# Summing the squares of a hidden state on TensorE alone instead of with VectorE's adds, and two small matmul loops written as one

## The chip, the cores and the metric

The kernel runs on one core of a Trainium2 chip. The metric is the device time of one execution in microseconds (us): before the change the median of three executions is 1692.14 us (1687.17 to 1692.53). Less is better.

## The reference

One inference step of a decoder layer over 512 prompt tokens and 32 sample tokens (8 sequences of 4 tokens), 544 token columns in all, in fp32. What matters here is the end of the layer and one place inside the RWKV-7 branch:

```
def rms_norm(x, g):
    xf = x.astype(jnp.float32)
    y = xf * lax.rsqrt(jnp.mean(xf * xf, axis=-1, keepdims=True) + RMS_EPS)
    return (y * g.astype(jnp.float32)).astype(x.dtype)

def merge_ffn(x, o_nsa, o_rwkv, o_mem, mg, ...):
    g = jax.nn.sigmoid(mg)                      # three gates per channel
    m = g[:, :, 0] * (o_nsa @ w_o_nsa) + g[:, :, 1] * (o_rwkv @ w_o_rwkv) + g[:, :, 2] * (o_mem @ w_o_mem)
    x = x + m @ w_out
    hf = rms_norm(x, ffn_norm)
    return x + (jax.nn.silu(hf @ w_gate) * (hf @ w_up)) @ w_down

y = rms_norm(merge_ffn(...), final_norm)

def rwkv_scan(s0, r, decay, k, v, kk, a):       # s: one 64 x 64 state per head
    sa = jnp.einsum('bhij,bhj->bhi', s, -kk_t)
    s = s * w_t + sa * (kk_t * a_t) + v_t * k_t
    y_t = jnp.einsum('bhij,bhj->bhi', s, r_t)
```

Both RMS norms need, for each token, the sum of squares over the 1024 channels. The RWKV branch is computed in chunks; the 32 sample tokens are the last chunk, and their two products with the old state (with r and with -kk) come from separately loaded states.

## The kernel before

Activations lie transposed, channels on the 128 partitions and tokens along the row: `x1T` holds the hidden state as 8 tiles (KT = 8) of 128 x 544. Each of the engines runs one long written-out program, and they are held together by counting semaphores; nothing reorders them. All weights stream through a ring of five slots in SBUF (`sb_ring`); each slot is 128 x 1024 fp32 (512 KB), serves eight 128 x 128 weight tiles, and is refilled by SyncE once its last matmul has counted up `slot_used`. PSUM is four accumulators `acc[0..3]` of two banks; a product over 544 tokens is two matmuls of 272 columns, one for each bank. In the trace an fp32 matmul call appears as two weight loads (LDWEIGHTS) and two MATMUL instructions, one for each pass.

The end of the layer has four stages: the branch outputs are projected and merged (L1599); the output projection (L1621), 8 tiles j of 16 matmul calls; gate and up of the feed-forward (L1641), 22 pairs of tiles; and the down projection (L1665, its last tile j = 7 at L1676), 8 tiles of 44 calls.

After output-projection tile j, VectorE adds it into `x1T` (`add(j)`, L2474), ScalarE makes the scaled copy `hT` (L2015) and the square `sqT` (L2011). The sum over the 8 tiles is then made by two engines. Square 0 goes into half 0 of `sqT`, squares 1 to 7 all into half 1. For j = 1 to 6 VectorE adds half 1 onto half 0 (`add_square`, L2480), counting `sq_added`, and ScalarE may write the next square only after that. TensorE then sums over the partitions with a 128 x 128 tile of ones: `square_sum(0)` for the half 0, `square_sum(1)` for square 7, each one call for each bank of `acc[3]` (L1610). ScalarE makes the reciprocal root from `acc[3]` (L2018, L2019). For the last norm the same is done with the down projection's tiles, and `square_sum(0)` and the halves of `square_sum(1)` stand inside and after the last tile, which is computed one bank after the other so that the final scaling (L2526) of the first 272 tokens can start early.

In the RWKV branch, TensorE also carries "fill" matmuls of the input projections (L935) between small matmuls that wait on other engines. For the sample chunk the state products `w_s` (64 x 64 for each head; 32 rows with r, 32 rows with z) are placed by identity matmuls: the z rows into `acc[1]` (L1147, weights: a 32 x 32 identity, 64 columns moving) and the r rows, turned, into `acc[2]` (L1151, weights: 32 x 64 of `w_s`, 32 columns moving). `crossed()` goes through the 12 heads with e (the half of the partitions) alternating. `from_uv` (L1052) adds onto `acc[1]` and waits for `ws_mm`, which the last L1151 counts.

Of the kernel before, what the change touches and what calls it, by code (L numbers as in the profile page):

```python
# [260 lines left out]
def program(nc, A):  # L261
    with ExitStack() as ctx:
# [166 lines left out]
        def r_z(feats, i, t0, n):  # L429
# [69 lines left out]
        mg_sig, mg_mm, mg_part, x1_added, sqT_made, sq_added, sqT_summed, rms_inv, hf_done, gu_scaled, gu_act, up_scaled, ff_done, dn_mm, out_stored = map(  # L499
            sem, ("mg_sig", "mg_mm", "mg_part", "x1_added", "sqT_made", "sq_added", "sqT_summed", "rms_inv",  # L500
# [351 lines left out]
        def _(pe):  # L852
# [292 lines left out]
            for e, s, k, i in crossed():  # L1145
                z_rows = slice(e * HD + TS, (e + 1) * HD)
                pe.matmul(acc[1][rows[1 - e], s, k * C:(k + 1) * C], ident[z_rows, z_rows], w_s[z_rows, i, :],  # L1147
                          start=k == 0, stop=False, skip_group_check=True)
            for e, s, k, i in crossed():
                r_rows = slice(e * HD, e * HD + TS)  # L1150
                mm = pe.matmul(acc[2][feats[e], s, k * C:k * C + TS], w_s[r_rows, i, :], ident[r_rows, r_rows],  # L1151
                               start=k == 0, stop=False, skip_group_check=True)
# [455 lines left out]
            def square_sum(x, halves=(0, 1)):  # L1608
                for b in halves:
                    mm = pe.matmul(acc[3][:, b, 0:HALF_T], ones, sqT[:, x, b * HALF_T:(b + 1) * HALF_T],  # L1610
                                   start=x == 0, stop=x == 1)
# [12 lines left out]
            pe.wait_ge(sq_added, KT - 2)  # L1624
            square_sum(0)
            pe.wait_ge(sqT_made, KT)
            square_sum(1)


# [26 lines left out]
            for j in range(KT - 1):  # L1656
                if j >= 2:
                    pe.wait_ge(x1_added, KT + j - 1)
                for k in range(FFT):
# [10 lines left out]
                    elif k == FFT - 1:  # L1670
                        mm.then_inc(dn_mm, 1)
            pe.wait_ge(x1_added, KT + KT - 2)
            for b in range(2):
                for k in range(FFT):
# [3 lines left out]
                    if b == 0 and k == FFT // 2:  # L1678
                        pe.wait_ge(sq_added, 2 * (KT - 2))
                        square_sum(0)  # L1680
                    if b == 1 and k == FFT // 2:
                        pe.wait_ge(sqT_made, 2 * KT)
                        square_sum(1, (0,))
                mm.then_inc(dn_mm, 1)
            pe.wait_ge(sqT_made, 2 * KT + 1)
            square_sum(1, (1,))

        @block.scalar
        def _(act):
# [318 lines left out]
            def square(j, done, cols=slice(0, T)):  # L2008
                if j >= 2:
                    act.wait_ge(sq_added, done * (KT - 2) // KT + j - 1)  # L2010
                act.activation(sqT[:, min(j, 1), cols], x1T[:, j, cols], ACT.Square).then_inc(sqT_made, 1)  # L2011
# [5 lines left out]
            act.wait_ge(sqT_summed, 2)  # L2017
# [18 lines left out]
            for b in range(2):  # L2036
# [3 lines left out]
                act.wait_ge(sqT_summed, 4 + b)  # L2040
# [6 lines left out]
        def _(dve):  # L2047
# [428 lines left out]
            def add_square(j, done):  # L2476
                dve.wait_ge(sqT_made, done + j + 1)
                if j >= 2:
                    dve.wait_ge(sq_added, done * (KT - 2) // KT + j - 1)
# [70 lines left out]
```

## Time and profile before

| | us |
|---|---|
| median of three executions | 1692.14 |
| the profiled execution | 1692.53 |
| its span, first to last instruction | 1690.7 |
| TensorE busy in it | 1605.8 (95%) |
| VectorE busy | 454.1 (27%) |
| ScalarE busy | 382.3 (23%) |

The profiled execution is the slowest of the three shown; 1.8 us of its time lie outside the span. Busy time of an engine is the union of its instructions. A matmul's duration in the trace is longer than its distance to the next, since matmuls are pipelined: 272 columns are listed with 392 ns, yet follow each other more closely. The page's groups are summed over the whole run; the order of events at one place is read from the timeline, and what released each step from the chain of waits.

### The profile page before, as it was taken

Reading aid. Unit: us, or ns where it says so; the run is one execution under the profiler, and the core shown is the slowest. Engines: PE = TensorE matmul, PEld = TensorE weight load, DVE = VectorE, ACT = ScalarE, POOL = GpSimd, SP = SyncE. Lnnn points to the kernel's source line nnn. Section 1 sums busy time; section 2 is a strip of 40 time slices with the busy share of each in tenths; the row PEclk is TensorE's granted clock in tenths of the full one; section 3 lists DMA queues with packets and bytes.
Section 4 is the critical chain, followed back from the end, with each engine's and each line's share of the span. In section 5 each row is a group of like instructions: output and inputs, shape, how many; then the busy total and the mean of one; then the engine's idle time right before and its main releaser. Section 6 shows DMA issues by size and latency. Waiting matters only on the chain.

```text
span 1690.7 us, 30991 instructions
## 1 busy us (share of the span) xinstructions
PE 1605.8 (95%) x13440; PEld 1250.0 (74%) x13440; DVE 454.1 (27%) x915; ACT 382.3 (23%) x730; POOL 103.2 (6%) x186
## 2 busy tenths in 40 slices
PE   6999999999999999998888779999999999999997
PEld 5888578867776767875556558878788888888886
DVE  2112005523223236314664242221111111110002
ACT  3011145122222214115665432001200000000002
POOL 0000000011001003005000310000000000000000
PEclk9999999999999999999999999999999999999999
DMA  5221353321101236436000875312222222222221
GB/s 206 73 75 62 112 196 98 112 58 40 38 25 41 78 110 205 129 120 193 10 1 9 274 265 192 128 65 73 66 71 75 75 70 67 74 75 74 65 75 53
DMA packets 56445, 161.79 MB, mean 96 GB/s; under 512 B 7136, under 2 KB 20544, under 8 KB 55136
## 3 DMA queue, kind: packets, MB, share of 16 engines
q1 hardware_dynamic: 47744, 120.87, 22.4%
q0 software_dynamic: 7136, 35.73, 6.2%
q10 hardware_dynamic: 1440, 3.33, 0.5%
q8 instruction: 102, 1.67, 0.4%
q14 instruction: 23, 0.19, 0.0%
HBM read 141.91 MB, written 22.15 MB: 97 GB/s over the span
## 4 chain that ended last, share of the span: by engine, by line
PE 89%; ACT 3%; issue 2%; SPq 2%; DVE 2%; DMA 1%; ACTq 0%; DVEq 0%
PE acc L1641 19%; PE acc L935 17%; PE acc L884 9%; PE acc L1665 8%; PE acc L1599 7%; PE acc L1621 3%; PE acc L921 2%; PE acc L1030 2%; PE acc L909 2%; PE acc L1384 1%; PE acc L1371 1%; PE acc L1395 1%; PE acc L1044 1%; SPq L630 1%; PE acc L1284 1%
## 5 line engine op out<-in xcount | busy, mean ns | idle before, releaser
L935 PE MATMUL acc<-sb_work,sb_ring 128*128 128x272 f32 x1280 | 333.3, 403 | 0.6 <-ACT sb_work L1748 0.6
L1641 PE MATMUL acc<-sb_work,sb_ring 128*128 128x272 f32 x1408 | 322.8, 392 | 0.0
L1641 PEld LDWEIGHTS acc<-sb_work,sb_ring 128*128 128x128 f32 x1408 | 267.5, 190 | 55.1
L935 PEld LDWEIGHTS acc<-sb_work,sb_ring 128*128 128x128 f32 x1280 | 231.4, 190 | 57.2 <-issue 10.4
L884 PE MATMUL acc<-sb_work,sb_ring 128*128 128x272 f32 x640 | 148.8, 396 | 3.8 <-DVE sb_work L2060 3.8
L884 PEld LDWEIGHTS acc<-sb_work,sb_ring 128*128 128x128 f32 x640 | 122.7, 192 | 29.7 <-issue 4.2
L1665 PE MATMUL acc<-sb_work,sb_ring 128*128 128x272 f32 x616 | 141.3, 392 | 0.0
L1665 PEld LDWEIGHTS acc<-sb_work,sb_ring 128*128 128x128 f32 x616 | 117.0, 190 | 24.1
L2025 ACT ACTIVATE sb_work<-sb_work (+1 forms) x22 | 14.4, 657 | 277.4 <-DVE sb_work L2498 277.4
L1748 ACT ACTIVATE sb_work<-acc 128x272 f32<-128x272 f32 x80 | 31.4, 394 | 163.0 <-PE acc L935 155.7
L2474 DVE TENSOR_TENSOR sb_work<-acc,sb_work 128x544 f32<-128x544 f32 (+1 forms) x17 | 11.7, 691 | 191.8 <-PE acc L1665 132.8
L1621 PE MATMUL acc<-sb_work,sb_ring 128*128 128x272 f32 x256 | 58.9, 393 | 1.7 <-DVEq L2469 1.7
L1794 ACT ACTIVATE sb_work<-acc 128x768 f32<-128x768 f32 (+3 forms) x50 | 37.1, 743 | 101.0 <-PE acc L1044 89.2
L1621 PEld LDWEIGHTS acc<-sb_work,sb_ring 128*128 128x128 f32 x256 | 48.6, 190 | 12.1 <-DVEq L2469 2.1
L2156 DVE TENSOR_TENSOR sb_work<-acc,sb_cst 128x384 f32<-128x384 f32 (+1 forms) x41 | 22.6, 552 | 129.5 <-PE acc L1030 129.5
L2500 DVE TENSOR_TENSOR sb_work<-acc,sb_work 128x544 f32<-128x544 f32 x22 | 15.9, 724 | 143.0 <-PE acc L1641 143.0
L2498 DVE TENSOR_TENSOR sb_work<-acc,sb_work 128x544 f32 (+1 forms) x22 | 15.9, 725 | 134.5 <-PE acc L1641 134.5
L2292 DVE TENSOR_REDUCE sb_small<-acc 128x2 f32<-128x256 f32 (+3 forms) x48 | 39.5, 824 | 35.3 <-PE acc L1374 35.3
L2011 ACT ACTIVATE sb_work<-sb_work 128x544 f32<-128x544 f32 (+1 forms) x17 | 10.6, 621 | 156.3 <-DVE sb_work L2480 98.2
L1599 PE MATMUL acc<-sb_onsaT,sb_ring 128*128 128x272 f32 x192 | 45.3, 392 | 0.0
L1599 PE MATMUL acc<-sb_work,sb_ring 128*128 128x272 f32 x192 | 45.3, 392 | 0.0
L1716 ACT ACTIVATE sb_work<-acc,sb_work 128x544 f32<-128x544 f32 x20 | 14.3, 713 | 132.2 <-PE acc L884 132.2
(376 smaller groups left out, 1898.3 us busy)
## 6 DMA issues: line engine op xcount, KB each, us to landing
sb_ring<-w_stream SPq DMA_DIRECT2D x158, 512.0 KB, 3.5
sb_work<-pages SPq DMA_DIRECT2D x64, 192.0 KB, 3.7
branch_gates<-sb_work SPq DMA_DIRECT2D x24, 272.0 KB, 4.4
sb_work<-branch_gates POOLq DMA_DIRECT2D x8, 816.0 KB, 14.6
sb_work<-mem_kT SPq DMA_DIRECT2D x8, 512.0 KB, 6.6
sb_work<-mem_v SPq DMA_DIRECT2D x8, 512.0 KB, 8.7
query_features<-sb_work SPq DMA_DIRECT2D x10, 272.0 KB, 4.3
sb_work<-x_T ACTq DMA_DIRECT2D x8, 272.0 KB, 4.7
```

The source lines that it names most:

```text
L884: mm = pe.matmul(acc[n % 4][:, b, 0:HALF_T], w[:, k, :], hT[:, k, b * HALF_T:(b + 1) * HALF_T], start=k == 0, stop=k == KT - 1)
L909: mm = pe.matmul(acc[n][:, h, :], memT[:, k, n * P:(n + 1) * P], w[:, 4 * h:4 * h + 4, :].rearrange("p a c -> p (a c)"), start=k == 0, sto ...
L921: mm = pe.matmul(acc[a][:, b, 0:HALF_T], lhsT, rhs[:, b * HALF_T:(b + 1) * HALF_T], start=True, stop=True)
L935: mm = pe.matmul(acc[3][:, half, 0:HALF_T], fill_w[0][:, k, :], hT[:, k, half * HALF_T:(half + 1) * HALF_T], start=k == 0, stop=k == KT - 1)
L1030: mm = pe.matmul(acc[0][rows[1 - e], s, k * C:k * C + n], gram[rows[e], par, e, i, n:2 * n], X(par, i)[rows[e], 0:n], start=True, stop=True)
L1599: mm = pe.matmul(acc[n % 4][:, b, 0:HALF_T], w[:, block % KT, :], x[:, b * HALF_T:(b + 1) * HALF_T], start=k == 0, stop=k == len(source) - 1)
L1621: mm = pe.matmul(acc[j % 2][:, b, 0:HALF_T], w[:, k, :], mT[:, k, b * HALF_T:(b + 1) * HALF_T], start=k == 0, stop=k == KT - 1)
L1641: mm = pe.matmul(acc[2 * x + n % 2][:, b, 0:HALF_T], w[:, k, :], hT[:, k, b * HALF_T:(b + 1) * HALF_T], start=k == 0, stop=k == KT - 1)
L1665: mm = pe.matmul(acc[j % 2][:, b, 0:HALF_T], w[:, block % KT, :], ffT[:, k, b * HALF_T:(b + 1) * HALF_T], start=k == 0, stop=k == FFT - 1)
L1748: act.activation(fill_now[:, f % 2, half * HALF_T:(half + 1) * HALF_T], acc[3][:, half, 0:HALF_T], ACT.Copy, scale=scale).then_inc(fill_ou ...
L1794: act.activation(XX[0:2 * n, c % 2, first:, :, 0:n], acc[0][0:2 * n, first:, 0:PAIRS * C].rearrange("p x (i c) -> p x i c", c=C)[:, :, :, ...
L2292: dve.tensor_reduce(small[:, c:c + 2], acc[u % 2][:, :, 0:(t + 1) * P], AX, ALU.max, negate=True)\
```

## The change

1. VectorE's `add_square` and the semaphore `sq_added` are gone. Square j goes to half j % 2 of `sqT`. TensorE calls `square_sum(j)` for every j, accumulating over eight calls for each bank in `acc[3]`: in the output projection after tile j + 1 (the last one after that of j = 6), in the down projection after tile j + 1 up to j = 5; `square_sum(6)` and the two halves of `square_sum(7)` keep their places in and after the last tile. ScalarE's square j waits until `square_sum(j - 2)` is done.
2. The two loops over `crossed()` at L1147 and L1151 become one, so that for each head the z matmul and then the r matmul are issued.

```diff
@@ -496,8 +496,8 @@
         wkv_sum = sem("wkv_sum")
         y_stored, in_back = sem("y_stored"), sem("in_back")
         spilled, sig_in = [sem("spilled0"), sem("spilled1")], [sem(f"sig_in{n}") for n in range(5)]
-        mg_sig, mg_mm, mg_part, x1_added, sqT_made, sq_added, sqT_summed, rms_inv, hf_done, gu_scaled, gu_act, up_scaled, ff_done, dn_mm, out_stored = map(
-            sem, ("mg_sig", "mg_mm", "mg_part", "x1_added", "sqT_made", "sq_added", "sqT_summed", "rms_inv",
+        mg_sig, mg_mm, mg_part, x1_added, sqT_made, sqT_summed, rms_inv, hf_done, gu_scaled, gu_act, up_scaled, ff_done, dn_mm, out_stored = map(
+            sem, ("mg_sig", "mg_mm", "mg_part", "x1_added", "sqT_made", "sqT_summed", "rms_inv",
                   "hf_done", "gu_scaled", "gu_act", "up_scaled", "ff_done", "dn_mm", "out_stored"))
         two = lambda name: [sem(f"{name}{n}") for n in range(2)]
         k_in, v_in, mk_in, mv_in = map(two, ("k_in", "v_in", "mk_in", "mv_in"))
@@ -1143,11 +1143,9 @@
             pe.wait_ge(ws_out, PAIRS)
             settle()
             for e, s, k, i in crossed():
-                z_rows = slice(e * HD + TS, (e + 1) * HD)
+                r_rows, z_rows = slice(e * HD, e * HD + TS), slice(e * HD + TS, (e + 1) * HD)
                 pe.matmul(acc[1][rows[1 - e], s, k * C:(k + 1) * C], ident[z_rows, z_rows], w_s[z_rows, i, :],
                           start=k == 0, stop=False, skip_group_check=True)
-            for e, s, k, i in crossed():
-                r_rows = slice(e * HD, e * HD + TS)
                 mm = pe.matmul(acc[2][feats[e], s, k * C:k * C + TS], w_s[r_rows, i, :], ident[r_rows, r_rows],
                                start=k == 0, stop=False, skip_group_check=True)
             mm.then_inc(ws_mm, 1)
@@ -1605,10 +1603,11 @@
                             mm.then_inc(mg_mm, 1)
 
 
-            def square_sum(x, halves=(0, 1)):
+            def square_sum(j, done, count=None, halves=(0, 1)):
+                pe.wait_ge(sqT_made, count or done + j + 1)
                 for b in halves:
-                    mm = pe.matmul(acc[3][:, b, 0:HALF_T], ones, sqT[:, x, b * HALF_T:(b + 1) * HALF_T],
-                                   start=x == 0, stop=x == 1)
+                    mm = pe.matmul(acc[3][:, b, 0:HALF_T], ones, sqT[:, j % 2, b * HALF_T:(b + 1) * HALF_T],
+                                   start=j == 0, stop=j == KT - 1)
                 mm.then_inc(sqT_summed, 1)
 
             pe.wait_ge(mg_part, 3 * KT + 1)
@@ -1621,10 +1620,9 @@
                         mm = pe.matmul(acc[j % 2][:, b, 0:HALF_T], w[:, k, :], mT[:, k, b * HALF_T:(b + 1) * HALF_T],
                                        start=k == 0, stop=k == KT - 1)
                 mm.then_inc(slot_used, 1)
-            pe.wait_ge(sq_added, KT - 2)
-            square_sum(0)
-            pe.wait_ge(sqT_made, KT)
-            square_sum(1)
+                if j:
+                    square_sum(j - 1, 0)
+            square_sum(KT - 1, 0)
 
 
             def ff_tile(n, it=None):
@@ -1669,6 +1667,8 @@
                         mm.then_inc(slot_used, 1)
                     elif k == FFT - 1:
                         mm.then_inc(dn_mm, 1)
+                if j:
+                    square_sum(j - 1, KT)
             pe.wait_ge(x1_added, KT + KT - 2)
             for b in range(2):
                 for k in range(FFT):
@@ -1676,14 +1676,11 @@
                     mm = pe.matmul(acc[1][:, b, 0:HALF_T], w[:, (block + k) % KT, :], ffT[:, k, b * HALF_T:(b + 1) * HALF_T],
                                    start=k == 0, stop=k == FFT - 1)
                     if b == 0 and k == FFT // 2:
-                        pe.wait_ge(sq_added, 2 * (KT - 2))
-                        square_sum(0)
+                        square_sum(KT - 2, KT)
                     if b == 1 and k == FFT // 2:
-                        pe.wait_ge(sqT_made, 2 * KT)
-                        square_sum(1, (0,))
+                        square_sum(KT - 1, KT, 2 * KT, (0,))
                 mm.then_inc(dn_mm, 1)
-            pe.wait_ge(sqT_made, 2 * KT + 1)
-            square_sum(1, (1,))
+            square_sum(KT - 1, KT, 2 * KT + 1, (1,))
 
         @block.scalar
         def _(act):
@@ -2006,15 +2003,15 @@
                 act.activation(sg, sg, ACT.Sigmoid).then_inc(mg_sig, 1)
 
             def square(j, done, cols=slice(0, T)):
-                if j >= 2:
-                    act.wait_ge(sq_added, done * (KT - 2) // KT + j - 1)
-                act.activation(sqT[:, min(j, 1), cols], x1T[:, j, cols], ACT.Square).then_inc(sqT_made, 1)
+                if done + j >= 2:
+                    act.wait_ge(sqT_summed, done + j - 1)
+                act.activation(sqT[:, j % 2, cols], x1T[:, j, cols], ACT.Square).then_inc(sqT_made, 1)
 
             for j in range(KT):
                 act.wait_ge(x1_added, j + 1)
                 act.activation(hT[:, j, :], x1T[:, j, :], ACT.Copy, scale=v("ffn", j)).then_inc(hf_done, 1)
                 square(j, 0)
-            act.wait_ge(sqT_summed, 2)
+            act.wait_ge(sqT_summed, KT)
             own(act.activation(h2(rms), acc[3][:, :, 0:HALF_T], ACT.Ln, scale=1.0 / D, bias=stat[:, 20:21]))
             act.activation(rms, rms, ACT.Exp, scale=-0.5).then_inc(rms_inv, 1)
 
@@ -2037,7 +2034,7 @@
                 cols = slice(b * HALF_T, (b + 1) * HALF_T)
                 act.wait_ge(x1_added, 2 * KT + b)
                 square(KT - 1, KT, cols)
-                act.wait_ge(sqT_summed, 4 + b)
+                act.wait_ge(sqT_summed, 2 * KT + b)
                 own(act.activation(rms[:, cols], acc[3][:, b, 0:HALF_T], ACT.Ln, scale=1.0 / D, bias=stat[:, 20:21]))
                 act.activation(rms[:, cols], rms[:, cols], ACT.Exp, scale=-0.5).then_inc(rms_inv, 1)
                 if b == 0:
@@ -2473,18 +2470,10 @@
                 x = h2(x1T[:, j, :])[:, columns, :]
                 dve.tensor_tensor(x, acc[j % 2][:, columns, 0:HALF_T], x, ALU.add).then_inc(x1_added, 1)
 
-            def add_square(j, done):
-                dve.wait_ge(sqT_made, done + j + 1)
-                if j >= 2:
-                    dve.wait_ge(sq_added, done * (KT - 2) // KT + j - 1)
-                dve.tensor_tensor(sqT[:, 0, :], sqT[:, 0, :], sqT[:, 1, :], ALU.add).then_inc(sq_added, 1)
-
             dve.wait_ge(in_back, 80)
             for j in range(KT):
                 dve.wait_ge(slot_used, S_OUT + j + 1)
                 add(j)
-                if j >= 2:
-                    add_square(j - 1, 0)
 
             dve.sem_inc(gu_scaled, 2)
             dve.sem_inc(up_scaled, 2)
@@ -2515,9 +2504,6 @@
                 else:
                     dve.wait_ge(dn_mm, j + 1 - (j + 1) // 4)
                 add(j)
-                if j >= 2:
-                    add_square(j - 1, KT)
-            add_square(KT - 2, KT)
 
             def final(b):
                 cols = slice(b * HALF_T, (b + 1) * HALF_T)
```

TensorE in the RWKV sample chunk, before. `acc1` and `acc2` are the PSUM accumulators, L935 the fill matmuls, L1052 `from_uv`; the last number pair is output partitions x columns.

```order
L935 MATMUL acc3<-sb_work,sb_ring 128x272 [waits fill_out]
L935 MATMUL acc3<-sb_work,sb_ring 128x272 x5
L1147 MATMUL acc1<-sb_work,sb_cst 32x64 [waits ws_out]
L1147 MATMUL acc1<-sb_work,sb_cst 32x64 x11
L1151 MATMUL acc2<-sb_cst,sb_work 64x32 x12
L1052 MATMUL acc1<-sb_work 32x64 [waits ws_mm]
```

The same place after the change, from the fill matmul on; the pair of rows with acc2 and acc1 goes on until each has stood 12 times, and then L1052 follows:

```order
L935 MATMUL acc3<-sb_work,sb_ring 128x272 [waits fill_out]
L935 MATMUL acc3<-sb_work,sb_ring 128x272 x5
L1147 MATMUL acc1<-sb_work,sb_cst 32x64 [waits ws_out]
L1149 MATMUL acc2<-sb_cst,sb_work 64x32
L1147 MATMUL acc1<-sb_work,sb_cst 32x64
```

The 12 matmuls into acc1 and the 12 into acc2, two runs before, now alternate one by one.

TensorE at the end of the output projection (L1621; `w_in_slot` is a slot of the weight ring, `x1_added` the add that frees the accumulator, `sq_added` an `add_square`), before:

```order
L1621 MATMUL acc0<-sb_work,sb_ring 128x272 [waits x1_added,w_in_slot0]
L1621 MATMUL acc0<-sb_work,sb_ring 128x272 x15
L1621 MATMUL acc1<-sb_work,sb_ring 128x272 [waits x1_added,w_in_slot1]
L1621 MATMUL acc1<-sb_work,sb_ring 128x272 x15
L1610 MATMUL acc3<-sb_work 128x272 [waits sq_added]
L1610 MATMUL acc3<-sb_work 128x272
L1610 MATMUL acc3<-sb_work 128x272 [waits sqT_made]
L1610 MATMUL acc3<-sb_work 128x272
L1646 UNCONDITIONAL_BRANCH [waits hf_done]
L1646 ISA
```

After (L1620 is the output projection, L1609 the sum of squares):

```order
L1620 MATMUL acc0<-sb_work,sb_ring 128x272 [waits x1_added,w_in_slot0]
L1620 MATMUL acc0<-sb_work,sb_ring 128x272 x15
L1609 MATMUL acc3<-sb_work 128x272 [waits sqT_made]
L1609 MATMUL acc3<-sb_work 128x272
L1620 MATMUL acc1<-sb_work,sb_ring 128x272 [waits x1_added,w_in_slot1]
L1620 MATMUL acc1<-sb_work,sb_ring 128x272 x15
L1609 MATMUL acc3<-sb_work 128x272 [waits sqT_made]
L1609 MATMUL acc3<-sb_work 128x272
L1609 MATMUL acc3<-sb_work 128x272 [waits sqT_made]
L1609 MATMUL acc3<-sb_work 128x272
L1644 UNCONDITIONAL_BRANCH [waits hf_done]
L1644 ISA
```

Where one pair of square sums waited for VectorE's `sq_added` and one for ScalarE's last square, there is now a pair behind every tile but the first, each behind a wait for a square, and two pairs behind the last tile.

VectorE in the output projection (L2474 `add`, L2480 `add_square`), before:

```order
L2464 TENSOR_TENSOR sb_work<-acc2,sb_work 128x544 [waits mg_mm]
L2468 TENSOR_TENSOR sb_work<-sb_work 128x544 [waits mg_part]
L2464 TENSOR_TENSOR sb_work<-acc3,sb_work 128x544 [waits slot_used,dve_own]
L2468 TENSOR_TENSOR sb_work<-sb_work 128x544 [waits mg_part]
L2474 TENSOR_TENSOR sb_work<-acc0,sb_work 128x544 [waits dve_own,slot_used,in_back]
L2474 TENSOR_TENSOR sb_work<-acc1,sb_work 128x544 [waits slot_used]
L2474 TENSOR_TENSOR sb_work<-acc0,sb_work 128x544 [waits slot_used]
```

After:

```order
L2461 TENSOR_TENSOR sb_work<-acc2,sb_work 128x544 [waits mg_mm]
L2465 TENSOR_TENSOR sb_work<-sb_work 128x544 [waits mg_part]
L2461 TENSOR_TENSOR sb_work<-acc3,sb_work 128x544 [waits slot_used,dve_own]
L2465 TENSOR_TENSOR sb_work<-sb_work 128x544 [waits mg_part]
L2471 TENSOR_TENSOR sb_work<-acc0,sb_work 128x544 [waits dve_own,slot_used,in_back]
L2471 TENSOR_TENSOR sb_work<-acc1,sb_work 128x544 [waits slot_used]
```

The adds onto the square sum, and with them VectorE's waits for `sqT_made`, have left the row; eight adds of the hidden state follow each other.

## Rows read from the trace of the kernel before

**Rows 1.** The page: the chain that ended last, share of the span by engine.

```profile
PE 89%; ACT 3%; issue 2%; SPq 2%; DVE 2%; DMA 1%; ACTq 0%; DVEq 0%
```

**Rows 2.** Stretches: busy us and (instructions) by engine, granted clock, DMA share, GB/s.

```profile
core 0: us, PE busy (x) PEld busy (x) DVE busy (x) ACT busy (x) POOL busy (x), PEclk, DMA share, GB/s
1131.70:1190.68 58.98, 58.93 (x256) 48.56 (x256) 8.23 (x12) 9.06 (x14) 0.00 (x0) 1.00 0.22 71
1194.04:1516.71 322.67, 322.67 (x1409) 267.52 (x1408) 46.36 (x64) 19.67 (x28) 0.00 (x0) 1.00 0.22 70
1516.71:1657.88 141.17, 141.17 (x618) 117.04 (x617) 8.32 (x12) 3.94 (x6) 0.00 (x0) 1.00 0.22 67
```

**Rows 3.** Chain that ended last, 600 to 760: start us, us, what.

```profile
627.81 0.79 PE acc L1147 x24
628.60 0.85 PE acc L1151 x23
...
629.58 0.86 PE acc L1052 x24
630.44 2.03 PE acc L935 x8
...
713.08 0.41 ACT sb_work L1748
...
733.07 5.39 DMA branch_gates<-sb_work
```

**Rows 4.** TensorE timeline from 627.7: start us, us, line, operands, tile, count.

```profile
627.74 0.47 PE L1147 MATMUL acc<-sb_work,sb_cst 32*32 32x64 f32 x10
...
628.27 0.33 PE L1147 MATMUL acc<-sb_work,sb_cst 32*32 32x64 f32 x6
628.53 0.24 PE L1151 MATMUL acc<-sb_cst,sb_work 32*64 32x32 f32 x1
```

**Rows 5.** Line L1147: durations ns min/median/max, first and last start.

```profile
L1147 PE MATMUL acc<-sb_work,sb_cst x24: 214/214/238, 627.7 to 628.4; 32*32 32x64 f32 x24
```

**Rows 6.** TensorE timeline, fill matmuls, then L1021 and L1022 in turns, first and last.

```profile
606.33 2.10 PE L935 MATMUL acc<-sb_work,sb_ring 128*128 128x272 f32 x8
608.36 0.21 PE L1021 MATMUL acc<-sb_cst,sb_work 32*32 32x32 f32 x1
608.36 0.21 PE L1022 MATMUL acc<-sb_work,sb_cst 32*32 32x32 f32 x1
...
608.79 0.19 PE L1022 MATMUL acc<-sb_work,sb_cst 32*32 32x32 f32 x1
```

**Rows 7.** Timeline at the end of the output projection.

```profile
1190.70 0.72 DVE L2474 TENSOR_TENSOR sb_work<-acc,sb_work 128x544 f32<-128x544 f32 x1 [5.98 <-PE acc L1621]
...
1191.34 0.71 DVE L2480 TENSOR_TENSOR sb_work<-sb_work 128x544 f32<-128x544 f32 x1
1191.46 0.75 ACT L2015 ACTIVATE sb_work<-sb_work,sb_vec 128x544 f32<-128x544 f32 x1 [6.04 <-DVE sb_work L2474]
...
1192.11 2.10 PE L1610 MATMUL acc<-sb_work 128*128 128x272 f32 x8 [1.45 <-DVE sb_work L2480]
1192.11 0.64 ACT L2011 ACTIVATE sb_work<-sb_work 128x544 f32<-128x544 f32 x1
...
1194.04 3.14 PE L1641 MATMUL acc<-sb_work,sb_ring 128*128 128x272 f32 x13
```

**Rows 8.** Timeline in the last tile of the down projection.

```profile
1663.38 1.08 PE L1610 MATMUL acc<-sb_work 128*128 128x272 f32 x4
...
1674.38 0.62 PE L1610 MATMUL acc<-sb_work 128*128 128x272 f32 x2
...
1677.30 3.39 DVE L2526 SCALAR_TENSOR_TENSOR sb_work<-sb_work,sb_vec 128x272 f32<-128x272 f32 x8 [7.78 <-ACT sb_work L2042]
```

**Rows 9.** SyncE's issues of weights in the output projection, and all by kind.

```profile
1139.51 14.99 SPq L612 DMA_DIRECT2D sb_ring<-w_stream  x3
...
sb_ring<-w_stream SPq DMA_DIRECT2D x158, 512.0 KB, 3.5
```

## The prediction

> **What bounds the kernel now.** I read the chain that ended last first: TensorE holds 89% of it and VectorE 2% [rows 1], so an instruction taken from VectorE is worth only the wait that it ends, and one given to TensorE is likely to be paid in full. Second, the stretches at the end of the layer. In the gate-and-up stage TensorE is busy 322.67 us of 322.67, in the down projection 141.17 of 141.17, in the output projection 58.93 of 58.98; the DMA engines are busy 0.22 of the time and the granted clock is 1.00, that is 2.4 GHz [rows 2]. TensorE has no gap there for anything to go into. VectorE works 8.2 to 8.3 us in each of the two projections. Third, the chain from 600 to 760 us: in the sample chunk both loops of the second edit stand on it, one behind the other and with fill matmuls after them, and it stays on TensorE's order until 713.08, where ScalarE and then SyncE's transfers take over, each started from there [rows 3]. What is added at 628 us arrives at the end. Last, the timelines of the three places.
>
> **The price of a square sum.** 1408 instructions in 322.67 us are 0.2292 us each, 616 in 141.17 us the same [rows 2]. A call is two instructions (the two passes of fp32), a `square_sum(j)` has two calls: 4 x 0.2292 = 0.917 us. The ones are loaded anew for each pass as every weight tile is, so nothing is saved or lost by that: at 1192.11 eight such instructions and at 1663.38 four run at this same distance [rows 7, 8].
>
> **Output projection.** Before, two square sums stand behind the last tile. After, there are eight, six of them between the tiles (behind j = 1 to 6) and two behind the last. The six cost 6 x 0.917 = 5.50 us. Do they wait? Square j is ready 2.05 us after tile j's result: add from 1190.70, copy, square until 1192.75 [rows 7]. TensorE asks for it one whole tile later, 32 x 0.2292 = 7.3 us, so no. Does ScalarE's new wait hold up anything? Square j wants `square_sum(j - 2)`, which TensorE has passed before it finished tile j; no. The refill of the ring slots: SyncE issues one in 5.0 to 7.5 us (three in 14.99 us, the first at its start), each lands 3.5 us later, and there are five slots [rows 9]; no.
>
> Behind the last tile a stall goes. Before, TensorE's sum waited 1.45 us, for VectorE's last `add_square` (1191.34 to 1192.05); from 1192.11 it worked to 1194.04 [rows 7]. After, `square_sum(6)` needs nothing of VectorE and goes into this wait. What is late next is square 7: it is behind the copy on ScalarE and ends at 1192.11 + 0.64 = 1192.75, its sum starts some 0.06 us later and takes 0.917, so gate and up start at 1193.73 instead of 1194.04: -0.3 us. If the removed add had held the square back as well (copy and add end together), this may be -0.4; if the restart costs more, 0. The first edit hence costs +5.2 here.
>
> **Down projection.** Before: `square_sum(0)` and the halves of `square_sum(1)`, in and behind the last tile. After: the same three places hold squares 6 and 7 and six more stand before them: +5.50 us. The sum at 1663.38 shows no idle time before it [rows 8], so no stall is there to win. From the last tile on TensorE's row is the same call for call, and the final chain (first half's sum at 1674.38, ScalarE, VectorE's scaling at 1677.30, then the second half) hangs on the same places of it [rows 8]: 0. The twelve VectorE adds of some 0.71 us that go (8.5 us) lie beside TensorE throughout, apart from the one above: 0.
>
> **The two loops made one.** Before: 24 instructions of L1147 from 627.74, 24 of L1151 from 628.53, then L1052 at 629.58: 1.84 us [rows 3, 4], 0.033 us for one within L1147. They follow each other so closely because e alternates and the two halves of the array work beside each other. At the seam they do not: the last L1147 starts at 628.27 + 0.33 - 0.214 = 628.386 and the first L1151 at 628.53, 0.144 us later [rows 4, 5]. That is 64 columns (64 x 0.2292 / 272 = 0.054) and about 0.09 more. The tile's shape changes there, from 32*32 to 32*64. The same 0.09 stands where the shape changes from 128*128 to 32*32: the last of eight fill matmuls starts at 606.33 + 2.10 - 0.39 = 608.04, L1021 at 608.36, 0.32 where 0.229 would do [rows 6]. After the change the shape changes at each of 24 calls instead of once. A call then has its two passes on one tile, 0.054 apart, and the change of 0.144 behind them: 24 x 0.198 = 4.75 us, less 1.84: +2.9, with some rounding up for the restarts +3.0. It is on the chain, and the fill matmuls behind it are in order behind it. Bounds: L1021 and L1022 alternate too, with one shape, and there 48 instructions start within 0.43 us [rows 6]; at that rate the edit would give 1.4. If every instruction ran alone, 48 x 0.214 [rows 5] = 10.3 us, +8.4. I take the value at the seam, since it is this pair of shapes itself.
>
> The Trainium skill speaks on both sides. "TensorEngine Tiling (Array Packing)", section "Tiling Modes", says that changing the tiling mode, not just the tile, drains the engine; it gives no time for it, and the trace's seam agrees. "TensorE: Matmul & The Clock Gate", "Part 3: Packing small matmuls", says that matmuls on different row groups run beside each other, a few ns apart; the merged loop has all four row groups in turns, so by this rule alone it should gain. The trace bears that out only for neighbours of one shape [rows 6].
>
> **Sum.** +5.2 + 5.5 + 0 + 3.0 = +13.7 us. The profiled execution of 1692.53 us (1690.7 of it span) becomes 1706.2; it lies 0.4 above the median, so the median goes to 1692.1 + 13.7 = 1705.8 us, 0.8% slower.
>
> **Rivals.**
> - A: the shapes do not matter, the four row groups run beside each other and L1151's half vanishes beside L1147's (-0.9). For it: L1021 and L1022. Against: the 0.144 at the seam. 5.2 + 5.5 - 0.9 = +9.8: 1701.9 us.
> - B: each change of shape costs clearly more when it is repeated, up to the bound of +8.4: for it, that one seam is all that shows this pair of shapes, and the second pass may restart late as well. Taking +6: 1708.8 us.
> - C, not slower: the square sums fall where TensorE would wait for weights, so the 11.0 us are hidden and only -0.3 and -0.9 are left: 1690.9 us. It decides once a slot's refill takes longer than the about 29 us that the four other slots give. Against it: landing in 3.5 us, DMA share 0.22 [rows 2, 9] and no idle time in the down projection.
> - D: a wait appears between the tiles, because ScalarE's square now waits for TensorE and TensorE for ScalarE. It costs from the point where 2.05 us exceed a tile of 7.3 us; if only the first waits slipped, each by 1 us, +6: 1712 us. The rows speak against it.
>
> **Chances.** Forecast 0.72, A 0.15, B 0.07, C 0.03, D 0.03. The range has to hold A and B, and the runs of the kernel before differ by up to 5 us (1687.17 the lowest), which may take a median of few runs down: 1698.5 to 1710. A change within 0.3% (5 us) cannot be told from none. Slower by more than that: forecast, A, B and D, less a small part for such low runs: 0.95; within 0.3%: 0.04; faster: 0.01.
>
> **What would show it.** In the changed profile: the output projection's stretch 5.5 us longer and the down projection's too, each with 24 more matmul instructions at 0.229 us and no idle time before them; VectorE with 12 instructions fewer; the wait behind the last output tile split, with square 7 the last to be waited for; the sample chunk's alternating rows lasting near 4.8 us, with starts 0.14 us apart where the shape changes. I am wrong if the two stretches grow by clearly less than 5 us, if TensorE waits at the square sums, or if the alternating rows last under 2 us or over 7.

## The result and the profile after

The changed kernel takes 1707.24 us (median of four executions, 1706.11 to 1710.62) against 1691.97 us before (also of four), 15.3 us more. Over all undisturbed executions, eleven of the changed kernel, the ratio is 1.0107, 95% interval 1.0086 to 1.0128: 18 us slower, between 15 and 22. The profiled execution took 1709.92 us with a span of 1708.1 us, 17.4 us more than the span before.

Where they went is read from TensorE's own row, cut at four places that both kernels have. The table gives the distances in us between the starts of matmuls; "first L1077" is the first matmul behind the fill that follows `from_uv`. "Again" is a second profile of the same kernel (the runs e7 and e8 below).

| stretch | before | before again | after | after again |
|---|---|---|---|---|
| start to first L1147 | 627.74 | 625.62 | 624.09 | 624.72 |
| first L1147 to first L1052 (the two loops, or one) | 1.84 | 1.84 | 6.05 | 6.48 |
| first L1052 to first L1077 (`from_uv` and 8 fill instructions) | 2.82 | 2.82 | 5.35 | 4.78 |
| first L1077 to the merge | 380.12 | 383.78 | 383.64 | 381.69 |
| merge to the last matmul | 669.36 | 669.37 | 680.15 | 680.15 |

The first and fourth stretch vary by up to 3.7 us between two profiles of the same kernel, so nothing in them can be put down to the change. Part of the fourth's variation is the clock, whose granted share is there at 0.50 for 17 to 28 us in pieces: 17.1 us in the profile of e3 below, where the stretch takes 379.6 us, 20.5 us in three profiles (380.1 to 382.2 us), 23.9 us in one (383.3) and 27.3 to 27.8 us in the five others (382.8 to 384.3). The other three stretches add +4.2, +2.5 and +10.8, in sum 17.5 us, and by the second pair of profiles +4.6, +2.0 and +10.8: the split between the loop and the piece behind it differs, the sum does not. That is the measured slowdown.

**The square sums.** The stretches of the changed kernel that answer to [rows 2], and two at the merged loop (same columns):

```profile
core 0: us, PE busy (x) PEld busy (x) DVE busy (x) ACT busy (x) POOL busy (x), PEclk, DMA share, GB/s
1138.32:1202.59 64.27, 64.27 (x280) 53.31 (x281) 5.08 (x7) 9.08 (x14) 0.00 (x0) 1.00 0.20 65
1205.92:1528.59 322.67, 322.67 (x1410) 267.52 (x1409) 46.40 (x64) 19.93 (x28) 0.00 (x0) 1.00 0.22 70
1528.59:1675.26 146.67, 146.67 (x642) 121.60 (x641) 6.52 (x9) 3.94 (x6) 0.00 (x0) 1.00 0.20 65
624.00:628.60 4.60, 4.60 (x42) 3.19 (x41) 0.00 (x0) 0.00 (x0) 0.00 (x0) 1.00 0.92 317
628.70:635.50 6.80, 6.65 (x42) 4.59 (x41) 0.55 (x1) 0.40 (x1) 0.00 (x0) 0.50 0.60 207
```

The output projection now has 280 instructions and TensorE is busy in all of its 64.27 us (58.77 before, with 256, if the stretch of [rows 2] is also taken from the first start, 1131.72, to where the next matmul was due, 1190.49: +5.50); the down projection up to the last tile has 24 more and takes 146.67 instead of 141.17; gate and up take 322.67 as before. Again there is no gap. The chain of waits of the changed kernel (start us, us, what) shows single pieces:

```profile
1187.17 7.33 PE acc L1620 x32
1194.51 0.92 PE acc L1609 x4
1195.42 7.35 PE acc L1620 x32
...
1204.90 1.18 PE acc L1609 x4
1206.08 322.67 PE acc L1639 x1408
```

Each square sum takes 0.92 us behind a tile of 7.33 us, and nothing is waited for between them. Behind the last output tile the timeline, which answers to [rows 7], reads:

```profile
1202.59 1.08 PE L1609 MATMUL acc<-sb_work 128*128 128x272 f32 x4
1202.79 0.72 DVE L2471 TENSOR_TENSOR sb_work<-acc,sb_work 128x544 f32<-128x544 f32 x1 [7.53 <-PE acc L1620]
...
1203.55 0.75 ACT L2012 ACTIVATE sb_work<-sb_work,sb_vec 128x544 f32<-128x544 f32 x1 [6.95 <-DVE sb_work L2471]
1204.21 0.64 ACT L2008 ACTIVATE sb_work<-sb_work 128x544 f32<-128x544 f32 x1
...
1204.90 1.18 PE L1609 MATMUL acc<-sb_work 128*128 128x272 f32 x4 [1.23 <-ACT sb_work L2008]
...
1205.92 1.31 PE L1639 MATMUL acc<-sb_work,sb_ring 128*128 128x272 f32 x5
```

The add has run beside `square_sum(6)`, which follows the tile at once, at 1202.59; the square of j = 7 ends at 1204.85 and its sum starts at 1204.90, so what is late is now ScalarE, as forecast. From the first of the sums to the first gate matmul it is 3.33 us. Before, the same distance from the end of the tile was 3.55 us (the next instruction was due at 1190.49, the gate matmul came at 1194.04). The end of the stall is worth 0.22 us. The second of the four instructions of the last sum starts 0.33 us behind the first and not 0.23, so that the sum takes 1.02 us from 1204.90 to the gate matmul (the chain's 1.18 holds the tail of a modelled duration as well).

**The merged loop.** TensorE's timeline there, which answers to [rows 4]:

```profile
621.70 2.45 PE L935 MATMUL acc<-sb_work,sb_ring 128*128 128x272 f32 x10
624.09 0.29 PE L1147 MATMUL acc<-sb_work,sb_cst 32*32 32x64 f32 x2
624.31 0.30 PE L1149 MATMUL acc<-sb_cst,sb_work 32*64 32x32 f32 x2
...
628.37 0.30 PE L1149 MATMUL acc<-sb_cst,sb_work 32*64 32x32 f32 x2
628.60 0.35 PE L1147 MATMUL acc<-sb_work,sb_cst 32*32 32x64 f32 x2
...
629.22 0.42 PE L1147 MATMUL acc<-sb_work,sb_cst 32*32 32x64 f32 x2
629.57 0.42 PE L1149 MATMUL acc<-sb_cst,sb_work 32*64 32x32 f32 x2
630.13 1.49 PE L1052 MATMUL acc<-sb_work 64*32 64x64 f32 x24
631.56 3.99 PE L935 MATMUL acc<-sb_work,sb_ring 128*128 128x272 f32 x8
635.48 0.70 PE L1077 MATMUL acc<-sb_work 32*32 32x64 f32 x18
```

Every row holds the two passes of one call, and the next call starts 0.22 to 0.23 us after it. A row lasts 0.29 with instructions of 0.214, so the second pass starts 0.08 us behind the first, and from there to the next call it is 0.144 us (from the z to the r matmul) or 0.147 us (back again), the seam of before. Calls with 64 columns and calls with 32 columns take the same. Then, from the row at 628.60 on, everything is slower: calls come 0.35 us apart, 24 instructions of L1052 take 1.49 us (0.86 before, [rows 3]), and eight fill instructions 3.99 (such eight last 2.10 us in [rows 6]). The last row of the stretches shows the clock there: from 628.7 to 635.5 us the granted clock is 0.50, that is 1.2 GHz, while it is 1.00 before the change throughout this part. What TensorE did before the clock fell: 4.6 us of single small matmuls with a change of shape between calls. After 635.5 the clock is back at 1.00.

### The profile page after: what moved, and what is told of

It reads as the page before. It is cut to its first block, busy times and chain, and to the rows that moved or that the text cites. A ratio compares the mean times of both kernels' runs of the same rounds, so it can differ in the third digit from the quotient of the medians.

```text
span 1708.1 us, 31067 instructions
## 1 busy us (share of the span) xinstructions
PE 1624.2 (95%) x13488; PEld 1263.8 (74%) x13488; DVE 446.7 (26%) x903; ACT 382.7 (22%) x730; POOL 103.5 (6%) x186
## 3 DMA queue, kind: packets, MB, share of 16 engines
q10 hardware_dynamic: 1440, 3.33, 0.5%
## 4 chain that ended last, share of the span: by engine, by line
PE 89%; ACT 3%; SPq 2%; issue 2%; DVE 2%; DMA 1%; ACTq 0%; DVEq 0%
PE acc L1639 19%; PE acc L935 17%; PE acc L884 9%; PE acc L1663 8%; PE acc L1597 7%; PE acc L1620 3%; PE acc L921 2%; PE acc L1030 2%; PE acc L909 2%; PE acc L1369 1%; PE acc L1382 1%; PE acc L1393 1%; PE acc L1044 1%; SPq L630 1%; PE acc L1282 1%
## 5 line engine op out<-in xcount | busy, mean ns | idle before, releaser
L935 PE MATMUL acc<-sb_work,sb_ring 128*128 128x272 f32 x1280 | 335.2, 405 | 1.0 <-ACT sb_work L1745 1.0
L935 PEld LDWEIGHTS acc<-sb_work,sb_ring 128*128 128x128 f32 x1280 | 232.5, 190 | 57.5 <-issue 10.2
L1620 PE MATMUL acc<-sb_work,sb_ring 128*128 128x272 f32 x256 | 59.9, 393 | 1.7 <-DVEq L2466 1.7
L1620 PEld LDWEIGHTS acc<-sb_work,sb_ring 128*128 128x128 f32 x256 | 48.6, 190 | 12.1 <-DVEq L2466 2.1
L2489 DVE TENSOR_TENSOR sb_work<-acc,sb_work 128x544 f32<-128x544 f32 x22 | 15.9, 725 | 142.9 <-PE acc L1639 142.9
L2487 DVE TENSOR_TENSOR sb_work<-acc,sb_work 128x544 f32 (+1 forms) x22 | 15.9, 725 | 134.8 <-PE acc L1639 134.8
```

Of the source, the lines that this page charges most:

```text
L935: mm = pe.matmul(acc[3][:, half, 0:HALF_T], fill_w[0][:, k, :], hT[:, k, half * HALF_T:(half + 1) * HALF_T], start=k == 0, stop=k == KT - 1)
L1620: mm = pe.matmul(acc[j % 2][:, b, 0:HALF_T], w[:, k, :], mT[:, k, b * HALF_T:(b + 1) * HALF_T], start=k == 0, stop=k == KT - 1)
```

## The experiments

All are set against the kernel before on the same chip. e1 to e4 share one set of its executions (median 1689.75 us), e5 to e8 another (1691.92 us).

**e1, the merged loop alone.** The kernel before, and the two loops made one as in the change's second part; the square sums stay.

> The kernel before with the two loops over the 12 heads made one, and nothing else of the change. Theory 1 (each of 24 changes of the tile's shape costs about 0.22 us, and behind this sparse stretch TensorE's granted clock falls to 0.5 for some 7 us, as in the changed kernel's profile): from the first L1147 to the first L1077 it takes 11.4 us where the kernel before takes 4.66, the clock is below 1.00 there, and the time rises by 5 to 7 us. Rival (the shape changes alone are the cost and the fall of the clock there was chance): 8.3 us from L1147 to L1077, clock 1.00, time +3.6 us. Rival A of the prediction (row groups pack): -0.9 us.

Measured: ratio 1.0056, interval 1.0039 to 1.0073 (+9.5 us, between 6.6 and 12.3). The loop takes 6.36 us, from the first L1052 to the first L1077 it is 4.98, together 11.34 (4.66 before): +6.7 us:

```profile
625.63 0.29 PE L1147 MATMUL acc<-sb_work,sb_cst 32*32 32x64 f32 x2
...
631.99 1.49 PE L1052 MATMUL acc<-sb_work 64*32 64x64 f32 x24
...
636.97 0.86 PE L1077 MATMUL acc<-sb_work 32*32 32x64 f32 x24
```

The stretches (columns as above) show the clock:

```profile
625.60:629.60 4.00, 4.00 (x37) 2.82 (x36) 0.00 (x0) 0.00 (x0) 0.00 (x0) 1.00 0.83 256
629.70:636.50 6.80, 6.65 (x44) 5.03 (x44) 0.55 (x1) 0.40 (x1) 0.00 (x0) 0.50 0.62 260
```

The trace gives theory 1's 11.4 us and its fall of the clock, and excludes both rivals. The timed slowdown is above the 5 to 7 us that I had given; its interval, from 6.6, just takes in the 6.7 us of the trace. What lies above 6.7 is likely the clock at other places. The mean granted clock of the six executions is 0.987 against 0.991 in the 17 of the kernel before. As an estimate, the share of the clock that was not granted, times the span, is 22.6 us here and 15.9 before: 6.7 us more, of which the fall at the loop (6.8 us at 0.50) makes 3.4. One of the other falls in this profile, from 353.2 to 356.7 us, comes long before the loop. Whether the edit has a part in the others is not shown.

**e2, the square sums alone.** The changed kernel with the two loops apart again:

```diff
             for e, s, k, i in crossed():
-                r_rows, z_rows = slice(e * HD, e * HD + TS), slice(e * HD + TS, (e + 1) * HD)
+                z_rows = slice(e * HD + TS, (e + 1) * HD)
                 pe.matmul(acc[1]..., ident[z_rows, z_rows], w_s[z_rows, i, :], ...)
+            for e, s, k, i in crossed():
+                r_rows = slice(e * HD, e * HD + TS)
                 mm = pe.matmul(acc[2]..., w_s[r_rows, i, :], ident[r_rows, r_rows], ...)
```

> The kernel before with the squares summed by TensorE alone, the two loops kept apart. Theory 1 (24 more instructions in each of two stages at 0.2292 us, nearly nothing won at the wait behind the last output tile): +10.9 us; the clock at 1.00 from 628 to 640 us. Rival (the new waits between ScalarE and TensorE cost as well, and make up what the prediction missed): +14 us or more, with idle time before the square sums.

Measured: ratio 1.0064, interval 1.0049 to 1.0079 (+10.8 us, between 8.3 and 13.3). From the merge to the last matmul it is 680.14 us (669.36 before): +10.8. The loops take 1.84 us, the piece behind them 2.82, and the clock stays up:

```profile
624.50:629.20 4.70, 4.53 (x81) 3.64 (x80) 0.55 (x1) 0.40 (x1) 0.00 (x0) 1.00 0.92 295
629.20:640.00 10.80, 10.76 (x86) 6.61 (x86) 7.76 (x12) 3.11 (x6) 4.65 (x7) 1.00 1.06 309
```

Theory 1 holds, with the price of the sums as worked out; no wait between the tiles costs anything. The ratios of e1 and e2 add up to 1.012, the change's is 1.0107.

**e3, fill in the middle of the merged loop.** As e1, with one edit more: four of the eight fill calls that stood ahead of the loop go into its middle.

```diff
-            fill((NCH, 7))
+            fill((NCH, 7), 0)
             pe.wait_ge(ws_out, PAIRS)
             settle()
-            for e, s, k, i in crossed():
+            for at_, (e, s, k, i) in enumerate(crossed()):
+                if at_ == 6:
+                    fill((NCH, 7), 1)
```

> As e1 (one loop over the heads), but the eight fill matmul calls ahead of the loop are parted: four stay ahead, four stand in its middle. The same work, with 16 dense matmul instructions less than 3 us away from any point of the sparse stretch. Theory 1 (the clock falls because TensorE had worked sparsely for some 5 us on end): the clock stays at 1.00 from the loop to L1077; from the first L1147 to the first L1077 it takes 4.66 + 1.83 (the moved fill) + 3.6 (shape changes) + 0.2 = 10.3 us, and the time is +3.8 us against before, about 3 us less than e1. Rival (the fall has another cause): the clock falls as in e1 and the piece takes 13 us.

Measured: ratio 1.0055, interval 1.0038 to 1.0072 (+9.3 us, between 6.4 and 12.2); 13.77 us from the first L1147 to the first L1077 (L1151 and L1079 in this kernel), which is +7.3 us once the old 4.66 and the moved fill's 1.83 are taken off. I was wrong here: the expected piece was 10.3 us. The clock (columns as above) falls twice:

```profile
626.60:630.30 3.70, 3.70 (x10) 2.42 (x8) 0.00 (x0) 0.00 (x0) 0.00 (x0) 0.54 0.93 306
630.30:633.00 2.70, 2.70 (x25) 1.91 (x24) 0.00 (x0) 0.00 (x0) 0.00 (x0) 1.00 1.06 451
633.40:637.00 3.60, 3.60 (x30) 2.85 (x28) 0.55 (x1) 0.36 (x1) 0.00 (x0) 0.53 0.14 58
637.00:642.00 5.00, 5.00 (x63) 3.80 (x62) 3.04 (x5) 0.85 (x3) 0.72 (x2) 1.00 0.59 164
```

and each time it is the work behind the sparse piece that pays, the fill in the middle, then `from_uv` and the fill behind it (L935 is L937 here, L1052 is L1054):

```profile
621.79 2.10 PE L937 MATMUL acc<-sb_work,sb_ring 128*128 128x272 f32 x8
...
626.62 3.79 PE L937 MATMUL acc<-sb_work,sb_ring 128*128 128x272 f32 x8
...
633.27 1.23 PE L1054 MATMUL acc<-sb_work 64*32 64x64 f32 x24
634.42 3.36 PE L937 MATMUL acc<-sb_work,sb_ring 128*128 128x272 f32 x8
```

Eight fill instructions last 2.10 us ahead of the loop, 3.79 in its middle and 3.36 behind it. This fill between the sparse pieces did not keep the clock up; it was only made slow itself. What is lost in the two falls, 1.7 us (3.79 less 2.10) and 1.6 us (1.23 less 0.86, and 3.36 less 2.10), is no less than the 2.9 us of the one fall of e1. My theory's "some 5 us on end" is refuted: the clock fell here behind pieces of 2.7 and 2.9 us. That it falls behind sparse matmuls stands.

**e4, one shape for all.** As e1, and the r matmul in two halves of 32 columns of weights:

```diff
-                mm = pe.matmul(acc[2][feats[e], s, k * C:k * C + TS], w_s[r_rows, i, :], ident[r_rows, r_rows],
-                               start=k == 0, stop=False, skip_group_check=True)
+                for half in range(0, HD, TS):
+                    mm = pe.matmul(acc[2][e * HD + half:e * HD + half + TS, s, k * C:k * C + TS],
+                                   w_s[r_rows, i, half:half + TS], ident[r_rows, r_rows],
+                                   start=k == 0, stop=False, skip_group_check=True)
```

> As e1, but each r matmul (32 x 64 weights, tile 32*64) is written as two of 32 x 32 weights, so that all 36 calls have the tile 32*32 and still alternate between acc1 and acc2. Theory 1 (the change of the tile's shape is what costs, not the alternation): the 72 instructions take 0.9 to 1.9 us from the first L1147 to the first L1052 (1.84 before, 6.04 in the changed kernel), the clock stays at 1.00, and the time is within 1 us of before. Rival (alternating between the two accumulators or between row groups costs by itself): 36 calls at 0.2 us, 7 us.

Measured: ratio 1.0005, interval 0.9993 to 1.0017. The 72 instructions, from 623.28 on, alternate between the accumulators as e1's do, and are through after 1.11 us, the timeline's last rows:

```profile
623.98 0.21 PE L1147 MATMUL acc<-sb_work,sb_cst 32*32 32x64 f32 x1
624.02 0.19 PE L1150 MATMUL acc<-sb_cst,sb_work 32*32 32x32 f32 x1
624.39 0.86 PE L1052 MATMUL acc<-sb_work 64*32 64x64 f32 x24 [0.18 <-PE acc L1150]
```

That is less than the 1.84 us of the two loops before, though there are 24 instructions more, and about a sixth of e1's 6.36. From L1052 to L1077 it is 2.82 us. So neither the alternation nor the two accumulators cost anything by themselves; with the changes of shape the 0.225 us for each call are gone, and so is the fall of the clock. It also shows that rival A's mechanism exists, once all tiles have one shape.

**e5, pairs of heads.** As e1, but two z matmuls, then two r matmuls:

```diff
-            for e, s, k, i in crossed():
+            heads12 = list(crossed())
+            for at_ in range(0, 12, 2):
+                for e, s, k, i in heads12[at_:at_ + 2]:
                     ...                                  # z matmul
+                for e, s, k, i in heads12[at_:at_ + 2]:
                     ...                                  # r matmul
```

> One loop again, but over pairs of heads (e = 0 and 1): two z matmuls, two r matmuls, and so on; 11 changes of shape inside it instead of 23. Theory 1 (shape changes are the price, two heads of a pair run beside each other): 12 pieces of 0.22 to 0.25 us, 2.6 to 3.0 us from the first L1147 to the first L1052. Then the clock: e3 showed it fall behind 2.7 us of sparse matmuls on either side of a fill. If length of the sparse piece decides, it falls here too, and from_uv to L1077 takes 4.3 us or more instead of 2.82; time +3 us against before. Rival (only one instruction at a time in the array brings the fall): clock 1.00, from_uv to L1077 2.82 us, time +1 us.

Measured: ratio 1.0009, interval 0.9995 to 1.0024. The loop takes 3.01 us, from L1052 to L1077 4.25. The timeline (L1149 is the z matmul here, L1153 the r matmul):

```profile
623.41 0.30 PE L1149 MATMUL acc<-sb_work,sb_cst 32*32 32x64 f32 x4
623.64 0.30 PE L1153 MATMUL acc<-sb_cst,sb_work 32*64 32x32 f32 x4
623.87 0.30 PE L1149 MATMUL acc<-sb_work,sb_cst 32*32 32x64 f32 x4
...
626.42 0.86 PE L1052 MATMUL acc<-sb_work 64*32 64x64 f32 x24 [0.16 <-PE acc L1153]
627.22 3.53 PE L935 MATMUL acc<-sb_work,sb_ring 128*128 128x272 f32 x8
630.68 1.06 PE L1077 MATMUL acc<-sb_work 32*32 32x64 f32 x24
```

Two calls of a pair now take the time of one (0.23 us a row), so the price is of the change of shape, not of the call. The stretches show the clock:

```profile
623.40:626.40 3.00, 2.86 (x49) 2.00 (x49) 0.00 (x0) 0.00 (x0) 0.00 (x0) 1.00 0.84 246
627.40:630.80 3.40, 3.40 (x12) 2.11 (x13) 0.55 (x1) 0.40 (x1) 0.00 (x0) 0.55 1.00 422
```

It is 1.00 in the loop and 0.55 behind it, so 1.4 us more are paid there: the rival is out, since two matmuls at a time did not keep the clock up. L1077, the last row of the timeline, takes 1.06 us instead of 0.86 and so pays another 0.2. By the trace it is +2.6 us up to the first L1077, +2.8 in all, which lies in the timed interval (-0.8 to +4.1 us).

**e6, a candidate.** Three edits on the kernel before: e4's loop; `add_square(6)` ahead of the last add; the last output-projection tile by banks (its counts on two semaphores that are free there):

```diff
+                order = [(k, b) for k in range(KT) for b in range(2)]
+                if j == KT - 1:
+                    order.sort(key=lambda x: x[1])
+                for k, b in order:
...
+            add_square(KT - 2, 0)
+            dve.wait_ge(ws_mm, PAIRS + 2)
+            add(KT - 1, slice(0, 1), ws_out)
+            dve.wait_ge(slot_used, S_OUT + KT)
+            add(KT - 1, slice(1, 2))
```

> The kernel before with (1) the loop of e4, all tiles 32*32, (2) VectorE's last add_square ahead of the last add, (3) the last output-projection tile computed one bank after the other, so that add, copy and square of its first 272 tokens run beside the second bank's matmuls. Theory: the loops give -0.7 us as in e4; behind the last tile the half add (0.44), copy and square (0.45 each) end 1.3 us after the last matmul instead of 2.05, and the wait for VectorE's add_square is gone: -0.9 us from the last tile's end to the first gate matmul. In all -1.6 us, 0.1%, at the edge of what the timing can tell. Rival (something else of the same chain is late, for instance ScalarE, which now has four short instructions there): no gain behind the last tile.

Measured: ratio 0.9995, interval 0.9982 to 1.0008; 1690.6 us against 1691.92. In the trace both gains are there: the loops take 1.11 us (-0.73), and behind the tile

```profile
1179.83 9.33 PE L1623 MATMUL acc<-sb_work,sb_ring 128*128 128x272 f32 x40
...
1188.99 1.08 PE L1610 MATMUL acc<-sb_work 128*128 128x272 f32 x4
...
1190.57 1.19 PE L1610 MATMUL acc<-sb_work 128*128 128x272 f32 x4 [0.49 <-ACT sb_work L2028]
...
1191.59 11.62 PE L1645 MATMUL acc<-sb_work,sb_ring 128*128 128x272 f32 x50
```

the gate matmuls start 2.83 us after the tile's last instruction (1179.83 + 9.33 - 0.39 = 1188.77, then 1191.59; 3.78 before, from 1190.27 to 1194.04): -0.95 us. From there to the last matmul 0.2 us are lost again (488.07 us against 487.84); the clock falls here at 1679.2, 0.5 us before the last matmul, and in the kernel before only after it. 1.7 us of 1692 cannot be told from nothing by the timing; it is faster by the trace only.

**e7 and e8, second profiles** of the kernel before and of the changed one.

> The kernel before once more, for a second profile. If the parts of the trace that the change does not touch (from the start to the first L1147, and from the first L1077 to the merge) vary by some us between two profiles of one kernel, then the -3.65 and +3.5 us that the changed kernel's profile shows there are chance. If they agree within 0.5 us, the change acts there too.

> The changed kernel once more, for a second profile. Theory 1: loops 6.0 us, from_uv to L1077 about 5.3 us with the clock at 0.5 again, merge to the last matmul 680.1 us; the rest varies as in e7. Rival (the fall of the clock at 628 us was chance): from_uv to L1077 takes 2.82 us here.

They took 1694.12 us and 1708.47 us, one execution each. Their distances stand in the first table. The stretch from L1077 to the merge differs by 3.7 us between the two profiles of the kernel before, and the first stretch by 2.1: by e7's first case, the -3.65 and +3.5 us of the changed kernel's profile are chance. The clock in e8:

```profile
624.70:628.40 3.70, 3.70 (x34) 2.63 (x34) 0.00 (x0) 0.00 (x0) 0.00 (x0) 1.00 0.89 264
628.50:635.30 6.80, 6.65 (x46) 5.04 (x45) 0.55 (x1) 0.40 (x1) 0.00 (x0) 0.50 0.64 265
```

In all three profiles that have the change's loop (after, e1, e8) it fell inside the loop, 3.8 to 4.6 us from its start, and for the same 6.8 us. In none of the five with the old loops or e4's did it fall there.

## Why the prediction was wrong

The direction was right and so was the price of the square sums; the total of +13.7 us was too small: +18 measured (15 to 22), which puts the time by the ratio at 1710.2 us, just above the range's upper end of 1710. The median of the first four executions, 1707.24 us, lies within the range; that it comes so near to the 1705.8 us forecast is luck, for the trace has 17.4 us more and not 13.7. Step by step:

- **What bounds the kernel**: right. What was added to TensorE came out in full, and twelve adds fewer on VectorE (903 instructions instead of 915) gave nothing but the stall behind the last tile.
- **The price of a square sum**, 0.917 us: right (0.92 each in the chain). The two terms of 5.50 us: right. With the stall, 10.8 us measured against 10.7.
- **The stall behind the last output tile**, -0.3: measured -0.22. Square 7 is late next, as the prediction said. The rest is the restart, which the prediction named: the last sum takes 1.02 us from start to start instead of 0.917.
- **The two loops made one**, +3.0: this is the step that failed; it is 6.7 (6.6 by the second profile). The price of the change of shape, 0.144 us from start to start, was right. Three things were missing. The second pass of a call was put 0.054 us behind the first, by the columns it streams, and it comes at 0.080 for both kinds of call, though the r matmul streams only half the columns: 0.6 us over 24 calls. The trace of the kernel before had this number, at the first call behind each change of shape: the second pass of the first L1147 starts 0.080 us after the first, that of the first L1151 0.079 us. Then L1052 follows the last r matmul at the old 0.38 us and not at 0.144. By these two alone, 23 distances of 0.2254 us, the last call's 0.08 and 0.38, the loop would take 5.65 us, +3.8 instead of +3.0. And the clock: from 628.7 to 635.5 us it is at 1.2 GHz, which costs the rest of the loop 0.4 us and the work behind it 2.5 (0.8 and 2.0 in e8). The prediction read the granted clock for the end of the layer alone, and treated the loop as work that has its own price and no effect on what stands behind it. e5 and e3 show that effect with other lengths of the sparse piece, e4 shows it gone with the change of shape.
- **The rivals**: A was refuted for this loop and confirmed for tiles of one shape (e4). B came nearest, with +6 for the loop and 1708.8 us. Its doubt that the second pass may restart late was right, but is worth 0.6 us; a change of shape did not cost more for being repeated (0.144 and 0.147 us until the clock fell), and the clock, most of what was missing, is not in it. C did not occur: the sums came out in full. D did not occur: there is no idle time before the sums between the tiles.
- **What would show it**: the two stretches grew by 5.50 us each and VectorE has 12 instructions fewer, as written. The alternating rows were to last near 4.8 us and last 6.05; until the clock fell there were 20 of the 24 in 4.5 us. The bound for being wrong there, 7 us, was set too wide to catch this, and no sign looked at the work behind the loop.

What exactly brings the clock down is open. These runs show only what TensorE did before it fell (2.7 and 2.9 us of single small matmuls with changes of shape in e3, 3.8 to 4.6 us of them in e8, e1 and the changed kernel, 3.0 us of paired ones in e5, there with `from_uv` and 0.5 us of fill behind them) and where it did not fall (1.84 or 1.11 us of packed ones). Length, sparseness and the changes of shape were not varied apart.

## What to carry to other kernels

Where TensorE has no gaps, work moved to it from an engine with 27% load is paid in full (11.0 us here), and the wait that it ends may give back little (0.22 us); count the instructions. Before two loops of small matmuls are merged, compare the tile shapes in the trace: where they differ, every alternation costs a change of shape (0.144 us from start to start here, where instructions of one shape followed each other at 0.033 on average), and the second pass of the call behind it comes late (0.080 us); where they are one shape, merging can gain (0.73 us by the trace of e4). Look at the first call behind a seam for the price, not at the average of a run. And ask of every sparse stretch what clock it leaves to the dense work behind it.

## What the runs showed of the hardware

- Between two changes of shape, 32*32 to 32*64 and back, a call takes 0.225 us, whether 64 or 32 columns stream through it, and a pair of calls on two halves of the array takes 0.23 us (e1, e5).
- 72 instructions of one tile shape, in turns on four groups of 32 rows, run through in 1.11 us, 15 ns each (e4); 48 in two runs of different shapes, each on two of the groups, took 1.84 us.
- A fall of the clock outlasts the sparse matmuls behind which it comes: in e3, dense fill matmuls between two sparse pieces ran at a granted clock of 0.54 (3.79 us for eight instead of 2.10) and did not prevent the second fall.
- Two profiles of one kernel differ by up to 3.7 us in a stretch that is the same code, so a single profile's difference there means nothing without a second one. The mean granted clock of each execution helps to judge such a difference: where the clock was at half for 27.3 us instead of 20.5, the stretch was 3.7 us longer (e7 against the first profile).
